# A gather ring of six slots instead of eight, and a half-chunk of query weights kept on chip between token blocks, in a two-layer decoder trunk

## The chip, the cores and the metric

The kernel runs on one core of a Trainium2 chip. The metric is the device time in microseconds (us) of one execution, all inputs in HBM, weights included. The kernel before took 1610.29 us in the median of three runs (1610.21, 1610.29 and 1612.72).

## The reference

A trunk of two layers runs over 256 tokens of width 1024, all in float32. Layer 0 mixes tokens with eight stick-breaking heads and four gated-linear-attention heads; layer 1 mixes them with a chunked gMLP gate (`c_w_in`, 1024 x 4096; a causal 128 x 128 matrix per group; `c_w_out`, 2048 x 1024). After each mixer comes a PEER block, and this is most of the work:

```
q = (h @ w_q)                                   # 1024 x 2048, 8 heads x 2 halves x 128
scores = einsum('thpd,hpnd->thpn', q, subkeys)  # 128 keys per half
top_s, top_i = top_k(scores, 16)                # per half, then the best 16 of the 16 x 16 sums
...
u_sel = u_tab[ii]                               # 128 experts per token, rows of 1024 floats
act = gelu(einsum('td,tkd->tk', xi, u_sel))
w = gi * act
out = einsum('tk,tkd->td', w, v_tab[ii])
```

Each token picks 128 of 16384 experts; of each it needs a row of `u` and a row of `v`, 8 KB together. Two layers and 256 tokens make 65536 such row pairs, 537 MB, gathered from HBM.

## The kernel before, in words

The 256 tokens are two blocks of 128, one token per partition. A *step* is one expert for each of a block's 128 tokens: 128 steps per block and layer, 512 in all, numbered 0 to 511 here over the four pairs (layer, block) = (0,0), (0,1), (1,0), (1,1). What a step does, engine by engine:

- POOL (L686) issues one indirect DMA that fetches 128 row pairs, 1 MB, into slot `t % SLOTS` of `ring` (8 slots of 8 KB per partition). Before it, POOL waits until step `t - SLOTS` has been used (`rows_used`), and in steps 2, 4, 6 and 7 of the whole kernel also for the end of what the prologue of layer 0 keeps in slots 4 to 7.
- DVE (L1229) multiplies the `u` half with the token's `h` and sums it to `dots`. It waits for all 16 parts of the DMA (`row_in`).
- ACT (L875, L876, L878) takes the gelu, multiplies by the gate and makes a diagonal 128 x 128 matrix of it.
- PE (L1580) multiplies that matrix with the `v` half into two PSUM banks, four matmul instructions, and counts `rows_used` up.

Everything else is placed between the steps by a list written out by hand, `PLAN`, which all five engines walk in the same order. `gather_with` puts stages behind given steps: the ranking of the next experts (`TOPK`, DVE), the query projection (`QPROD` and `QMORE`, PE) with its keys (`QDOT`), and layer 1's mixer (`ZPROJ`, `MIXG`, `MIXT`, `MIXO`), of which block 0 is computed behind the steps of (0,1) and block 1 behind those of (1,0). An engine never passes what stands ahead of it in this list.

Weights are streamed. A chunk is 1024 x 512 (2 MB), loaded by SP in two halves of 1 MB (`load_chunk`, L561). Each half goes to a *room* of 8 KB per partition: rooms 0 to 3 in `weights`, 4 in `scores1`, 5 and 6 in `z`, 7 and 8 in `more`. Rooms 4 to 8 are free only in parts of the plan (`spans`). `weight_rooms` walks the plan before the program is built and gives each half the room that has been free longest; SP then waits, in the order of the plan, until the last use of that room is over, and issues the load. A half listed in `kept` and `kept_halves` stays in its room (it is *pinned*) from block 0's use until block 1's, and block 1 then loads nothing. Kept so far are `ZPROJ` 2 and 3 and layer 1's query parts 2 and 3; layer 1's query parts 0 and 1 are loaded for each block anew. Layer 0's query parts serve both blocks from one load.

SP also loads the keys of layer 1 (`QKEYS`), after the last key product of layer 0, and nothing behind them in its order can be issued before.

Gathers (POOL's queue) and weight loads (SP's queue) are served by the same 16 DMA engines.

Of the kernel before, what the change touches and what calls it, by code (L numbers as in the profile page):

```python
# [5 lines left out]
P = 128  # L6
NBLK = 2
T = P * NBLK
D = 1024
KT = D // P  # L10
CH = 512
# [8 lines left out]
NEG = -1.0e30  # L20
LOWEST = -3.0e38

SLOTS = 8
STEPS = NE
PARTS = 4
PHEADS = PH // PARTS
# [1 line left out]
WB = 4  # L28
# [4 lines left out]
BATCHES = 6  # L33
# [54 lines left out]
ALL = tuple(range(PHEADS))  # L88
# [4 lines left out]
LOW_ROOMS = ((0, 1), (2, 3))  # L93
SCORES_ROOM, Z_HIGH_ROOM, Z_LOW_ROOM = 4, 5, 6
MORE_ROOMS = (7, 8)
N_ROOMS = 9
TK_PARTS = 6


# [186 lines left out]
def weight_rooms():  # L286

    places = {stage: at for at, stage in enumerate(PLAN)}
    last_mix = [max(places["MIXT", b, k] for k in range(4)) for b in range(NBLK)]
    spans = {SCORES_ROOM: [(places["TOPK", 0, 1, PH - 1, TK_PARTS - 1], places["VEC", "final", 0])]}  # L290
    for room in MORE_ROOMS:
        spans[room] = [(places["GLAREAD", 1], len(PLAN))]
    for room in (Z_HIGH_ROOM, Z_LOW_ROOM):
        spans[room] = [(last_mix[0], places["ZTAKE", 1, Z_ORDER[1][0]]), (last_mix[1], len(PLAN))]
    kept = {("ZPROJ", 1, 3): ("ZPROJ", 0, 3), ("ZPROJ", 1, 2): ("ZPROJ", 0, 2),
            ("QPROD", 1, 1, 2, ALL): ("QPROD", 1, 0, 2, ALL), ("QPROD", 1, 1, 3, ALL): ("QPROD", 1, 0, 3, ALL)}
    kept_halves = {("ZPROJ", 0, 3): (0, 1), ("ZPROJ", 0, 2): (0, 1), ("QPROD", 1, 0, 2, ALL): (0, 1), ("QPROD", 1, 0, 3, ALL): (0, 1)}
    again = {first: (later[0], later[1:]) for later, first in kept.items()}
    used_until, fills, pinned, homes = [-1] * N_ROOMS, [0] * N_ROOMS, set(), {}
    rooms, numbers, fresh = [], [], []  # L300
    for kind, args, at in walk():
        for i in range(chunks_of(kind, args)):
            name, n = (kind, *args), len(rooms)
            uses = half_uses(kind, args, places)
            place, number, new = [], [], []
            for half in range(2):
                if uses is None:
                    room, wait = 2 * (n % 2) + half, "used"
                    used_until[room] = places["OUT", 1, i, 3] if kind == "WOUT" else places[name]
                elif name in kept and half in kept_halves[kept[name]]:  # L310
                    room, wait = homes[kept[name]][half], None
                    pinned.discard(room)
                    used_until[room] = uses[half]
                else:
                    begin, end = places[name], uses[2 * i + half]
                    until = half_uses(*again[name], places)[half] if half in kept_halves.get(name, ()) else end
                    if kind == "MIXO" and i:
                        begin = places["OMORE", *args, 4]
                    choice = []
                    for r in range(N_ROOMS):  # L320
                        free_from, ok = used_until[r], r < SCORES_ROOM
                        for a, z in spans.get(r, ()):
                            if a < begin and until < z:
                                free_from, ok = max(free_from, a), True
                        if ok and free_from < begin and r not in pinned:
                            choice.append((free_from, r))
                    forced = name == ("ZPROJ", 0, 2) and half == 0
                    free_from, room = max(choice, key=lambda c: c[1]) if forced else min(choice)
                    wait = "used" if used_until[room] == free_from else "span"
                    used_until[room] = end  # L330
                if wait:
                    fills[room] += 1
                place.append(room)
                number.append(fills[room])
                new.append(wait)
                if half in kept_halves.get(name, ()):
                    pinned.add(room)
            rooms.append(place)
            numbers.append(number)
            fresh.append(new)  # L340
            homes[name] = place
    return rooms, numbers, fresh


ROOMS, FILLS, LOADS = weight_rooms()
# [6 lines left out]
BANKS = {}  # L352
# [7 lines left out]
def trunk(nc, x_in, cols, ab_w_in, ab_w_rank, ab_w_alpha2, ab_w_out, c_w_in, c_spatial, c_w_out,  # L360
# [6 lines left out]
    with ctx:  # L367
        def sb(name, shape, dt=f32):
            return ctx.enter_context(nc.sbuf_tensor(name, shape, dt))
# [8 lines left out]
        mixT = sb("mixT", [P, KT, T])  # L378
        weights = sb("weights", [P, 2, KT, CH])
        more = sb("more", [P, 2, KT // 2, CH])  # L380
        ring = sb("ring", [P, SLOTS, 2 * D])
        z = sb("z", [P, 2 * SGW])
        scores = sb("scores", [P, 2 * PH * NK])
        scores1 = sb("scores1", [P, 2 * PH * NK])
# [36 lines left out]
        def slots(k, n=1):  # L421
# [1 line left out]

        wide_rooms = [weights[:, i // 2, i % 2 * 4:i % 2 * 4 + 4, :] for i in range(4)] + [
            tile.rearrange("p (k n) -> p k n", n=CH) for tile in (scores1[:, :], z[:, SGW:2 * SGW], z[:, 0:SGW])] + [
            more[:, i] for i in range(2)]
        more_rows = more[:, :, :, :].rearrange("p a k n -> p (a k n)")
        first_chunk = z[:, :].rearrange("p (k n) -> p k n", n=CH)

# [30 lines left out]
        full = [sem(f"bank_full{k}") for k in range(WB)]  # L460
# [29 lines left out]
        sums_full = sem("sums_full")  # L490
# [50 lines left out]
        def _(sp):  # L541
# [6 lines left out]
            def load_chunk(n, src, used, block=0):  # L548

                for half in range(2):  # L550
                    room = ROOMS[n][half]
                    if LOADS[n][half] == "span" and room == SCORES_ROOM:
                        sp.wait_ge(experts_ready, 1 + IDS_ORDER[0, 1, PH - 1])
                    elif LOADS[n][half] == "span" and room in MORE_ROOMS:
                        sp.wait_ge(*filled(BANKS["GLAREAD", 1]))
                    elif LOADS[n][half] == "span":
                        sp.wait_ge(*filled(max(BANKS["MIXT", block, k] for k in range(4))))
                    elif LOADS[n][half] and room in room_used:
                        sp.wait_ge(*room_used[room])
                    if LOADS[n][half]:  # L560
                        sp.dma_start(wide_rooms[room], src[:, 4 * half:4 * half + 4, :]).then_inc(chunk_in[room], 16)  # L561
                    room_used[room] = used[half]

            for kind, args, at in walk():
# [43 lines left out]
                elif kind == "MIXO":  # L608
                    b, n = args
# [12 lines left out]
        def _(pool):  # L622
# [31 lines left out]
            for kind, args, at in walk():  # L654
                bank, chunk = at.bank, at.chunk
                if kind == "CAUSAL":
                    pool.wait_ge(spatial_in, 16)
                    pool.affine_select(out=spatialT[:, :, :], in_=spatialT[:, :, :], compare_op=ALU.is_ge, fill=0.0, base=0,
                                       pattern=[[0, SGG], [1, P]], channel_multiplier=-1).then_inc(spatial_masked, 1)
                elif kind == "GS":  # L660
                    for b in range(NBLK):
                        n = bank + b
                        pool.wait_ge(free[n % WB], n // WB + 1)

                        pool.affine_select(out=scT[:, b], in_=scT[:, b], compare_op=ALU.is_ge, fill=0.0, base=0,  # L665
                                           pattern=[[0, GH], [1, P]], channel_multiplier=-1).then_inc(scores_masked, 1)
                        pool.wait_ge(scores_masked, 2 * b + 1)
                        pool.memset(scT[0:GC, b, :, GC:P], 0.0).then_inc(scores_masked, 1)
                elif kind == "GATHER":
                    layer, b, i0, i1 = args  # L670
                    for step in range(i0, i1):
                        t = first_step(layer, b) + step
                        pool.wait_ge(experts_ready, 1 + IDS_ORDER[layer, b, step // TOPK])
                        if t == 2:
                            n = BANKS["GV", 1]
                            pool.wait_ge(full[n % WB], n // WB + 1)
                        elif t == 4:
                            pool.wait_ge(scores_full, BATCHES)
                        elif t == 6:
                            pool.wait_ge(sums_full, BATCHES)  # L680
                        elif t == 7:
                            n = BANKS["GLAREAD", 1]
                            pool.wait_ge(full[n % WB], n // WB + 1)
                        if t >= SLOTS:
                            pool.wait_ge(rows_used, t - SLOTS + 1)
                        pool.indirect_dma_start(  # L686
                            ring[:, t % SLOTS, :], None, uv_rows,
                            bass.IndirectOffsetOnAxis(ap=experts[:, b, step:step + 1], axis=0))\
                            .then_inc(row_in[t % SLOTS], 16)
# [964 lines left out]
```

## Time and profile before

| quantity | before |
|---|---|
| median of three runs | 1610.29 us |
| span of the profiled execution | 1611.4 us |
| PE, DVE, ACT, POOL busy | 89%, 61%, 41%, 41% |
| moved by DMA | 626.57 MB, mean 389 GB/s |
| gathers | 512 issues, 536.90 MB |
| loads and stores of the other queues | 89.6 MB |

The profiled execution's own time is given as its span, from its first instruction to the end of its last: 1611.4 us, inside the range of the three runs and 1.1 us over their median. The profile cuts the span into 40 slices of 40.3 us; in most of them from the fifth on DMA moves 421 or 422 GB/s.

### The profile page before, as it was taken

The numbers are of one execution on the slowest core, as the hardware profiler recorded it, in microseconds if no ns is written. First come the engines' busy times: TensorE is split into PE (matmuls) and PEld (weight loads), VectorE is DVE, ScalarE is ACT, GpSimd is POOL, SyncE is SP. The second block draws the span as 40 slices with busy tenths as digits, with TensorE's granted clock in tenths as the row PEclk, the third lists the DMA queues.
The fourth block names the chain that finished last, engine by engine and source line by source line (L and its number), as shares of the span: only waits on it lengthen the run. The fifth ranks groups of instructions, "written<-read, shape, count | busy, mean of one in ns | idle before, by whom it ended". The sixth has DMA issues, their size and how long they took to land.

```text
span 1611.4 us, 14849 instructions
## 1 busy us (share of the span) xinstructions
PE 1434.2 (89%) x4450; PEld 706.0 (44%) x4450; DVE 980.2 (61%) x2487; ACT 668.2 (41%) x1841; POOL 654.7 (41%) x535
## 2 busy tenths in 40 slices
PE   7999989999957998998988999999899889797776
PEld 6546455465412433443343545445335345342222
DVE  1226578758748756753347756566556778777744
ACT  1514544534525334442244534343334454444433
POOL 1001344444434333353345333333344544556673
PEclk9999999999989999999999999999999999999999
DMA  5443999999999999999999999999999999999996
GB/s 212 158 155 129 422 421 422 421 421 421 421 422 421 393 423 421 421 422 421 422 419 407 422 421 421 421 422 373 423 421 409 422 420 401 421 421 421 421 421 280
DMA packets 86656, 626.57 MB, mean 389 GB/s; under 512 B 9760, under 2 KB 9904, under 8 KB 10672
## 3 DMA queue, kind: packets, MB, share of 16 engines
q0 software_dynamic: 73728, 536.90, 80.6%
q1 hardware_dynamic: 12672, 88.45, 13.5%
q8 instruction: 35, 0.57, 0.1%
q14 instruction: 45, 0.37, 0.1%
q10 hardware_dynamic: 176, 0.28, 0.1%
HBM read 624.54 MB, written 1.05 MB: 388 GB/s over the span
## 4 chain that ended last, share of the span: by engine, by line
PE 42%; DMA 33%; DVE 10%; ACT 6%; issue 4%; POOL 3%; SPq 0%; POOLq 0%; DVEq 0%; ACTq 0%
DMA ring<-in_peer_uv,experts 33%; PE acc L1580 22%; DVE ring L1229 6%; PE work L1367 5%; PE work L1350 5%; POOL ring L686 3%; PE work L1339 3%; PE work L1382 2%; PE acc L1543 1%; ACT diag L878 1%; ACT gelus L876 1%; ACT L875 1%; PE work L1434 1%; ACT gelus L875 1%; ACT L869 1%
## 5 line engine op out<-in xcount | busy, mean ns | idle before, releaser
L1580 PE MATMUL acc<-ring,diag 128*128 128x512 f32 x2048 | 979.0, 612 | 158.7 <-ACT diag L878 156.6
L686 POOL DMA_INDIRECT ring<-in_peer_uv,experts x512 | 645.3, 1260 | 845.1 <-PE acc L1580 700.3
L1229 DVE CUSTOM_DVE_ANT_0 ring<-ring,h 128x1024 f32<-128x1024 f32 x512 | 624.9, 1226 | 440.4 <-DMA ring<-in_peer_uv,experts 427.8
L1580 PEld LDWEIGHTS acc<-ring,diag 128*128 128x128 f32 x2048 | 367.7, 191 | 687.5 <-ACT diag L878 349.5
L875 ACT ACTIVATE gelus<-dots 128x1 f32<-128x1 f32 x512 | 103.2, 201 | 694.5 <-DVE dots L1229 693.9
L878 ACT ACTIVATE diag<-ident,gelus 128x128 f32<-128x128 f32 x512 | 205.5, 401 | 16.7
L876 ACT ACTIVATE gelus<-gelus,gates 128x1 f32<-128x1 f32 x512 | 150.8, 295 | 16.6
L1350 PE MATMUL work<-weights,hT 128*128 128x512 f32 x192 | 88.1, 592 | 0.0
L1367 PEld LDWEIGHTS work<-hT,weights 128*128 128x128 f32 x576 | 69.8, 192 | 16.3 <-issue 16.3
L1367 PE MATMUL work<-hT,weights 128*128 128x128 f32 x576 | 70.1, 275 | 0.0
L1350 PEld LDWEIGHTS work<-weights,hT 128*128 128x128 f32 x192 | 36.2, 191 | 43.1 <-issue 43.0
L875 ACT ACT_TABLE_LOAD x41 | 52.6, 1283 | 0.7
L1350 PE MATMUL work<-more,hT 128*128 128x512 f32 x104 | 49.1, 594 | 0.0
L1339 PE MATMUL work<-hT,weights 128*128 128x256 f32 x192 | 43.5, 389 | 1.1 <-DMA weights<-in_ab_w_in 1.1
L1229 DVE DVE_READ_ACCUMULATOR2_ANT dots<- 128x1 f32 x512 | 42.2, 82 | 0.0
L1339 PEld LDWEIGHTS work<-hT,weights 128*128 128x128 f32 x192 | 37.6, 196 | 7.2 <-issue 1.9
L869 ACT ACT_TABLE_LOAD x31 | 39.8, 1283 | 0.5
L665 POOL TENSOR_SCALAR_AFFINE_SELECT more<-more 128x512 f32<-128x512 f32 x2 | 1.3, 630 | 88.1 <-ACT more L825 88.1
L1367 PEld LDWEIGHTS work<-hT,z 128*128 128x128 f32 x256 | 31.0, 192 | 7.2 <-issue 6.2
L1367 PE MATMUL work<-hT,z 128*128 128x128 f32 x256 | 31.6, 275 | 0.8 <-ACT hT L728 0.8
L1350 PEld LDWEIGHTS work<-more,hT 128*128 128x128 f32 x104 | 19.9, 193 | 24.5 <-issue 24.5
L1543 PE MATMUL acc<-weights,mixT 128*128 128x512 f32 x64 | 29.5, 595 | 0.8 <-DVE mixT L1181 0.8
(211 smaller groups left out, 898.3 us busy)
## 6 DMA issues: line engine op xcount, KB each, us to landing
weights<-in_c_w_in SPq DMA_DIRECT2D x14, 1024.0 KB, 9.1
more<-in_c_w_in SPq DMA_DIRECT2D x11, 1024.0 KB
weights<-in_ab_w_in SPq DMA_DIRECT2D x10, 1024.0 KB, 5.2
weights<-in_peer_w_q SPq DMA_DIRECT2D x10, 1024.0 KB, 9.2
ring<-in_peer_uv,experts POOLq DMA_INDIRECT x512
weights<-in_ab_w_out SPq DMA_DIRECT2D x4, 1024.0 KB, 5.2
weights<-in_c_w_out SPq DMA_DIRECT2D x4, 1024.0 KB, 12.2
scores<-in_c_w_out SPq DMA_DIRECT2D x4, 1024.0 KB
```

Of the source, the lines that this page charges most:

```text
L686: pool.indirect_dma_start(ring[:, t % SLOTS, :], None, uv_rows, bass.IndirectOffsetOnAxis(ap=experts[:, b, step:step + 1], axis=0))\
L869: nc.scalar.activation(g, g, ACT.Exp).then_inc(gate_exp, 1)
L875: link(nc.scalar.activation(gelus[:, k:k + 1], dots[:, k:k + 1], ACT.Gelu))
L876: link(nc.scalar.activation(gelus[:, k:k + 1], gelus[:, k:k + 1], ACT.Copy, scale=gates[:, b, step:step + 1]))
L878: nc.scalar.activation(diag[:, k, :], ident[:, :], ACT.Copy, scale=gelus[:, k:k + 1])\
L1229: nc.vector.tensor_tensor_reduce(out=ring[:, k, 0:D], in0=ring[:, k, 0:D], in1=h[:, b, :], scale=1.0, scalar=0.0, op0=ALU.mult, op1=ALU.ad ...
L1339: last = nc.tensor.matmul(dst, wt[k][:, t * P:(t + 1) * P], hT[:, k, cols], start=(k == 0), stop=(k == KT - 1))
L1350: last = nc.tensor.matmul(w[:, :], src[:, k, b * P:(b + 1) * P], wt[k], start=(k == 0), stop=(k == KT - 1))
L1367: last = nc.tensor.matmul(w[:, i * P:(i + 1) * P], wt[k][:, t * P:(t + 1) * P], hT[:, k, b * P:(b + 1) * P], start=(k == 0), stop=(k == KT ...
L1382: last = nc.tensor.matmul(w[:, :], mixT1[:, kh * KT + k % KT, :], wt[k % KT], start=(k == 0), stop=(k == 2 * KT - 1))
L1543: last = nc.tensor.matmul(acc[2 * b + n][:, :], mixT[:, k, b * P:(b + 1) * P], wt[k], start=(k == 0), stop=(k == KT - 1))
L1580: last = nc.tensor.matmul(acc[2 * b + n][:, :], diag[:, k, :], ring[:, k, D + n * CH:D + (n + 1) * CH], start=False, stop=True, skip_group ...
```

## The change

The ring has six slots. The two slots taken from it become rooms 9 and 10 for half-chunks of weights, free from stage `GLAREAD` 1 on (until then the prologue uses that memory, as before). The two halves of layer 1's query part 1 are kept from block 0 to block 1. The two waits of POOL that protected the old slots 6 and 7 go, and SP waits for `GLAREAD` 1 before the first fill of rooms 9 and 10. `dots`, `gelus`, `diag` and the semaphores `row_in` shrink to six with `SLOTS`.

```diff
-SLOTS = 8
+SLOTS = 6
+RING_ROOMS = 2
...
-N_ROOMS = 9
+SLOT_ROOMS = (9, 10)
+N_ROOMS = 11
...
-    for room in MORE_ROOMS:
+    for room in MORE_ROOMS + SLOT_ROOMS:
         spans[room] = [(places["GLAREAD", 1], len(PLAN))]
...
-    kept = {("ZPROJ", 1, 3): ("ZPROJ", 0, 3), ("ZPROJ", 1, 2): ("ZPROJ", 0, 2),
+    kept = {("QPROD", 1, 1, 1, ALL): ("QPROD", 1, 0, 1, ALL), ("ZPROJ", 1, 3): ("ZPROJ", 0, 3), ("ZPROJ", 1, 2): ("ZPROJ", 0, 2),
             ("QPROD", 1, 1, 2, ALL): ("QPROD", 1, 0, 2, ALL), ("QPROD", 1, 1, 3, ALL): ("QPROD", 1, 0, 3, ALL)}
-    kept_halves = {("ZPROJ", 0, 3): (0, 1), ...
+    kept_halves = {("QPROD", 1, 0, 1, ALL): (0, 1), ("ZPROJ", 0, 3): (0, 1), ...
...
-        ring = sb("ring", [P, SLOTS, 2 * D])
+        ring = sb("ring", [P, SLOTS + RING_ROOMS, 2 * D])
...
-            more[:, i] for i in range(2)]
+            more[:, i] for i in range(2)] + [
+            ring[:, SLOTS + i, :].rearrange("p (k n) -> p k n", n=CH) for i in range(RING_ROOMS)]
...
-                    elif LOADS[n][half] == "span" and room in MORE_ROOMS:
+                    elif LOADS[n][half] == "span" and room in MORE_ROOMS + SLOT_ROOMS:
                         sp.wait_ge(*filled(BANKS["GLAREAD", 1]))
...
                         elif t == 4:
                             pool.wait_ge(scores_full, BATCHES)
-                        elif t == 6:
-                            pool.wait_ge(sums_full, BATCHES)
-                        elif t == 7:
-                            n = BANKS["GLAREAD", 1]
-                            pool.wait_ge(full[n % WB], n // WB + 1)
                         if t >= SLOTS:
                             pool.wait_ge(rows_used, t - SLOTS + 1)
```

## Rows read from the trace of the kernel before

**Rows 1.** The page, parts 1 and 2: busy time; GB/s in 40 slices.
```profile
PE 1434.2 (89%) x4450; PEld 706.0 (44%) x4450; DVE 980.2 (61%) x2487; ACT 668.2 (41%) x1841; POOL 654.7 (41%) x535
...
GB/s 212 158 155 129 422 421 422 421 421 421 421 422 421 393 423 421 421 422 421 422 419 407 422 421 421 421 422 373 423 421 409 422 420 401 421 421 421 421 421 280
```
**Rows 2.** The page, part 3: DMA queues, packets, MB, share of 16 engines.
```profile
q0 software_dynamic: 73728, 536.90, 80.6%
q1 hardware_dynamic: 12672, 88.45, 13.5%
```
**Rows 3.** The page, part 4: the chain that ended last, by engine.
```profile
PE 42%; DMA 33%; DVE 10%; ACT 6%; issue 4%; POOL 3%; SPq 0%; POOLq 0%; DVEq 0%; ACTq 0%
```
**Rows 4.** Timeline of DVE in the last stretch: start, us, form [idle before, releaser].
```profile
1549.60 1.22 DVE L1229 CUSTOM_DVE_ANT_0 ring<-ring,h 128x1024 f32<-128x1024 f32 x1 [1.26 <-DMA ring<-in_peer_uv,experts]
...
1552.08 1.22 DVE L1229 CUSTOM_DVE_ANT_0 ring<-ring,h 128x1024 f32<-128x1024 f32 x1 [1.25 <-DMA ring<-in_peer_uv,experts]
```
**Rows 5.** Timeline of POOL in the same stretch.
```profile
1554.64 1.97 POOL L686 DMA_INDIRECT ring<-in_peer_uv,experts  x1 [0.52 <-issue]
```
**Rows 6.** Timeline of SP around 1180 us.
```profile
1171.29 8.91 SPq L561 DMA_DIRECT2D z<-in_peer_w_q  x2
1188.46 0.33 SPq L561 DMA_DIRECT2D scores<-in_peer_w_q  x1
```
**Rows 7.** The page, part 6: KB each, median us from issue to landing.
```profile
weights<-in_ab_w_out SPq DMA_DIRECT2D x4, 1024.0 KB, 5.2
```
**Rows 8.** Windows around 540 us: length, busy of PE, PEld, DVE, ACT, POOL, PEclk, DMA, GB/s.
```profile
538.50:539.50 1.00, 1.00 (x4) 0.51 (x3) 0.93 (x2) 0.98 (x2) 0.42 (x1) 1.00 0.45 188
539.50:542.40 2.90, 2.90 (x9) 1.23 (x8) 2.83 (x7) 2.79 (x6) 0.80 (x1) 1.00 0.99 364
542.40:543.40 1.00, 1.00 (x4) 0.52 (x3) 0.86 (x6) 0.89 (x4) 0.14 (x1) 1.00 0.52 164
```
**Rows 9.** Timeline of POOL in five stretches: the late issues.
```profile
260.39 1.65 POOL L686 DMA_INDIRECT ring<-in_peer_uv,experts  x1 [2.05 <-PE acc L1580]
...
537.98 0.94 POOL L686 DMA_INDIRECT ring<-in_peer_uv,experts  x1 [4.58 <-PE acc L1580]
541.60 0.94 POOL L686 DMA_INDIRECT ring<-in_peer_uv,experts  x1 [2.68 <-PE acc L1580]
...
1107.30 1.89 POOL L686 DMA_INDIRECT ring<-in_peer_uv,experts  x1 [2.11 <-PE acc L1580]
...
1238.16 1.49 POOL L686 DMA_INDIRECT ring<-in_peer_uv,experts  x1 [2.57 <-PE acc L1580]
...
1333.41 1.96 POOL L686 DMA_INDIRECT ring<-in_peer_uv,experts  x1 [9.04 <-PE acc L1580]
```
**Rows 10.** Timeline of DVE in the same stretches: starts that a landing released.
```profile
264.98 1.23 DVE L1229 CUSTOM_DVE_ANT_0 ring<-ring,h 128x1024 f32<-128x1024 f32 x1 [1.25 <-DMA ring<-in_peer_uv,experts]
...
519.84 1.23 DVE L1229 CUSTOM_DVE_ANT_0 ring<-ring,h 128x1024 f32<-128x1024 f32 x1 [0.84 <-DMA ring<-in_peer_uv,experts]
...
1095.82 1.23 DVE L1229 CUSTOM_DVE_ANT_0 ring<-ring,h 128x1024 f32<-128x1024 f32 x1 [0.18 <-DMA ring<-in_peer_uv,experts]
...
1112.23 1.22 DVE L1229 CUSTOM_DVE_ANT_0 ring<-ring,h 128x1024 f32<-128x1024 f32 x1
...
1237.61 1.22 DVE L1229 CUSTOM_DVE_ANT_0 ring<-ring,h 128x1024 f32<-128x1024 f32 x1 [1.25 <-DMA ring<-in_peer_uv,experts]
...
1337.63 1.23 DVE L1229 CUSTOM_DVE_ANT_0 ring<-ring,h 128x1024 f32<-128x1024 f32 x1 [0.54 <-DMA ring<-in_peer_uv,experts]
```
**Rows 11.** Windows of the trunk stages, the same columns.
```profile
550.00:721.00 171.00, 162.17 (x407) 72.77 (x406) 107.99 (x280) 71.98 (x199) 68.49 (x57) 0.99 1.01 421
721.00:824.00 103.00, 88.72 (x210) 37.21 (x207) 40.40 (x68) 32.47 (x100) 39.59 (x33) 0.98 1.01 421
...
1190.00:1226.00 36.00, 31.05 (x103) 15.72 (x103) 21.03 (x40) 16.47 (x46) 15.23 (x12) 0.95 1.01 421
```
**Rows 12.** Waits of PE between 565 and 1250 us, longest first.
```profile
PE acc L1580 <- ACT diag L878: 52.5, 53, 3.0
```

More of the change, by code:

```diff
@@ L294, in weight_rooms @@
         spans[room] = [(last_mix[0], places["ZTAKE", 1, Z_ORDER[1][0]]), (last_mix[1], len(PLAN))]
-    kept = {("ZPROJ", 1, 3): ("ZPROJ", 0, 3), ("ZPROJ", 1, 2): ("ZPROJ", 0, 2),
+    kept = {("QPROD", 1, 1, 1, ALL): ("QPROD", 1, 0, 1, ALL), ("ZPROJ", 1, 3): ("ZPROJ", 0, 3), ("ZPROJ", 1, 2): ("ZPROJ", 0, 2),
             ("QPROD", 1, 1, 2, ALL): ("QPROD", 1, 0, 2, ALL), ("QPROD", 1, 1, 3, ALL): ("QPROD", 1, 0, 3, ALL)}
-    kept_halves = {("ZPROJ", 0, 3): (0, 1), ("ZPROJ", 0, 2): (0, 1), ("QPROD", 1, 0, 2, ALL): (0, 1), ("QPROD", 1, 0, 3, ALL): (0, 1)}
+    kept_halves = {("QPROD", 1, 0, 1, ALL): (0, 1), ("ZPROJ", 0, 3): (0, 1), ("ZPROJ", 0, 2): (0, 1), ("QPROD", 1, 0, 2, ALL): (0, 1), ("QPROD", 1, 0, 3, ALL): (0, 1)}
     again = {first: (later[0], later[1:]) for later, first in kept.items()}
```

## The prediction

> **What bounds the kernel now.** I read the page's parts 1 and 2 first. PE is busy 89% of the span, which looks like the bound, but the line of GB/s says otherwise: from the fifth slice of 40.3 us to the last but one it stands at 421 or 422, whatever stage the plan is in, with dips in a few slices only [rows 1]. Nothing computes at so even a rate; this is the rate at which DMA can go here, and 1 MB (1.0486 million bytes) takes 1.0486 / 0.421 = 2.49 us. The gathers are 536.9 of the 625.4 MB of the two big queues, the weights most of the rest [rows 2]. The chain of waits gives PE 42% and DMA 33% [rows 3]; it hops between the two because each gather waits for a matmul to free its slot and each matmul for a gather. So I looked at one turn of this loop in the last stretch, where little else runs. DVE starts 2.49 us apart, each time released by a landing [rows 4]. Step 491 lands at 1549.60 and POOL issues the gather that reuses its slot at 1554.64: 5.04 us for dot product, diagonal matrix, matmuls and release. The issue itself stands there 1.97 us [rows 5]. A turn of eight slots is 8 x 2.49 = 19.9 us, so 19.9 - 5.04 - 1.97 = 12.9 us lie between the end of an issue and its landing, five transfers' time. The queue is deep, and DMA alone sets the end. Every byte less is time less, as long as DMA never waits for an issue.
>
> **The change, part by part.**
>
> *Two loads less.* Layer 1's query part 1 is no longer loaded for block 1. Its halves are the second of the two loads issued from 1171.29 us on and the one at 1188.46 [rows 6] (the first of the pair still belongs to part 0). They lie in the saturated stretch: 2 x 2.49 = 5.0 us gained.
>
> *Two more rooms.* In layer 0 the weights can come two halves earlier, in layer 1 the two new rooms are outweighed by the two pinned halves. The same bytes go through the same engines, only earlier; I cost it at nothing, and what it costs if PE minds is a rival below. SP's order is unchanged, and behind the key load of layer 1 nothing can be issued early anyway. POOL loses two waits near step 6. There gather 6 will wait for step 0 instead, some 6 us later than before; the two halves that now come with the first loads after the prologue keep DMA busy meanwhile, and PE is behind there, not DMA. Nothing.
>
> *The shorter ring.* A turn is now 6 x 2.49 = 14.9 us. In the last stretch 14.9 - 5.04 - 1.97 = 7.9 us are left from issue to landing. What is the least that does? A transfer of 1 MB to idle DMA engines lands 5.2 us after its issue starts [rows 7], of which the issue takes 0.3: 4.9 us is one end. The other comes from 540 us, where before already most DMA engines had run dry: POOL's issue ends at 538.92 (the row of 537.98 in [rows 9]), DMA is at half rate until about 539.5, busy for 2.9 us, and falls to half again at 542.4 [rows 8]. The gather's data were through 3.5 us after the end of the issue, and the signal comes after that. I take 4.2, the middle. So in the last stretch nothing is lost (4.2 against 7.9), and DMA runs dry only where PE frees a slot late.
>
> Where is that? The dips of [rows 1] mark four places (the slices from 524, 1088, 1209 and 1329 us), and I went through POOL's issues for more. In the shorter ring the slot freed at a given moment takes the gather two numbers lower, so an issue of before, with its time, now carries the gather two before it. It is late if the end of the issue + 4.2 lies after the time at which that lower gather landed before. POOL's rows are [rows 9], landings [rows 10], counted on by 2.49 us a step where DVE was late and does not show them:
> - Step 40 issued 260.39 + 1.65 + 4.2 = 266.2; step 38 landed at 264.98: 1.3 us late.
> - Step 144: 541.60 + 0.94 + 4.2 = 546.7; step 142, ten after the landing at 519.84, at 544.7: 2.0. The next issues are late by no more, since SP issues a weight half in this place, and its transfer fills the hole.
> - Step 330: 1107.30 + 1.89 + 4.2 = 1113.4; step 328, by pace 1110.8, at the latest when DVE took it, 1112.2: 1.2 to 2.6. The slice holds the deepest dip, so landings were behind the pace: 1.2.
> - Step 371: 1238.16 + 1.49 + 4.2 = 1243.9; step 369 at 1237.61 + 5.0 = 1242.6: 1.3.
> - Step 408: 1333.41 + 1.96 + 4.2 = 1339.6; step 406 at 1337.63: 1.9.
>
> Each hole shifts all later landings, which gives the engines behind a rest but is never won back; between the places PE catches up, so the next starts from zero and the five add: 7.7 us. With 3.5 us in place of 4.2 it would be 4.2 us; with 4.9, and 2.6 at step 330, it would be 12.6 plus some 1.5 for four or five issues that stand just short of late: 14.1.
>
> **Sum.** -5.0 + 7.7 = +2.7 us, between -0.8 and +9.1. The profiled execution's span, 1611.4, lies 1.1 over the median of the runs; the sum is a difference, small against both, so I put it on the median: 1610.3 + 2.7 = **1613.0 us**.
>
> **The rivals.**
>
> *The idle engine is served sooner, and most of the saving stays.* POOL's rows are 0.94 us long in some places and up to 1.96 in others [rows 9]. If the long ones only report the work late, a gather lands 0.94 + 3.5 = 4.4 us after its start, however long the row. Then the five places give 0, 1.3, 0, 0 and 0.2: 1.5 us lost, -5.0 + 1.5 = -3.5, **1606.8 us**. For it: the dip at 540 is served fast. Against it: the landing signal must come after the last byte, and 5.2 for the loads is longer. The Trainium skill, page "DMA: Bandwidth & Descriptors", section "Anatomy of one DMA — SWDGE (gpsimd) path", speaks for this side: about 2.0 us fixed plus bytes / 436 GB/s, 4.4 us for 1 MB, mostly the receipt of the last write. The 5.2 us of rows 7 are 0.8 longer than that rule gives.
>
> *The ring is too shallow in more places.* Places near the limit decide: the time from landing to reissue may be at most 14.9 - 4.2 less the issue's 0.9 to 2. If a restart takes 4.9 us or more, or if the pauses make PE fall to the half clock, the near places open too: +9 and more, **1619.4 us**. For it: DMA already thins out in five slices with eight slots. Against it: a thin slice is made of engines ahead of the others, and landings kept their pace.
>
> *The trunk is PE's.* From 550 to 721 us PE is busy 162.2 of 171.0, from 721 to 824 88.7 of 103.0, and 31.1 of 36.0 just after the loads that go [rows 11]. Weights that come earlier leave a stretch of bare gathers at 2.49 us a step later, where PE has less time for its projections; and the pinned halves may make a later half wait. PE waits today in these stages for nothing but the diagonal matrices [rows 12], so it has no stall of this kind that could shrink. If the 5 us taken from around 1180 are not all slack of PE's, up to those 5 us come back on top: -5.0 + 7.7 + 5.0, **1618 us**.
>
> **How the numbers follow.** 0.2% (3.2 us) is what a measurement of this kernel can tell from no change. Forecast 0.52, own range 1609.5 to 1617; first rival 0.25; second 0.15; third 0.08. Faster by over 3.2 us: nearly all of the first rival and a sliver of the forecast, 0.24. Within 3.2: two thirds of the forecast and the rest of the first rival, 0.36. Slower by over 3.2: the rest, 0.40. The range from 1606 to 1620 takes in the first rival's time and the upper bound.
>
> **What would show it.** In the last stretch issue to landing should be near 7.9 us and landings 2.49 apart. DMA bytes fall by 2.1 MB to 624.5. GB/s falls at the same five places, more than before, and DVE starts behind landings there instead of behind its own work. I am wrong if the last stretch itself goes slower than 2.49 us a step (the least from issue to landing is then over 7.9), if dips appear in slices that had none, or if PE shows waits for weights.

## The result, and the profile after

The changed kernel takes 1630.76 us (median of four runs, 1630.07 to 1633.46) against 1611.51 for the kernel before in the same comparison. The ratio is 1.0123, 95% interval 1.0111 to 1.0135: 19.2 us slower. The forecast was 1613.0 us, with a range to 1620. The direction was given the largest chance, the size was wrong by a factor of seven. Two of the eleven executions of `keep_one` below (1678.90 and 2536.88 us) were slow ones at a lower granted clock; they are left out of its time and ratio.

The page of the changed kernel, the lines that answer to [rows 1 to 3]:

```profile
PE 1442.2 (89%) x4450; PEld 707.1 (43%) x4450; DVE 981.9 (60%) x2487; ACT 669.1 (41%) x1841; POOL 660.5 (41%) x535
...
GB/s 209 170 141 158 420 392 394 422 413 409 421 422 404 390 422 421 421 406 420 422 420 422 363 423 417 422 421 373 422 415 382 419 392 364 422 412 416 421 421 313
...
q1 hardware_dynamic: 12384, 86.35, 13.1%
...
PE 45%; DMA 28%; DVE 12%; ACT 5%; issue 5%; POOL 5%; SPq 0%; POOLq 0%; DVEq 0%; ACTq 0%
```

The engines' work is the same. The two loads are gone: 2.1 MB less on the second queue. But the even row of 421 GB/s has more holes: from the fifth slice to the last but one, seventeen lie under 420 GB/s where there were six, and the chain goes less through DMA and more through engines. Dips in slices that had none (392 and 394 in the sixth and seventh from the start) were one of the forecast's signs of being wrong. The loads of layer 1's query weights near 1180 us, against [rows 6] (timeline of SP):

```profile
1170.97 0.33 SPq L564 DMA_DIRECT2D ring<-in_peer_w_q  x1
1181.24 0.33 SPq L564 DMA_DIRECT2D z<-in_peer_w_q  x1
```

Two half-chunks where there were four in this part of the plan; those of part 1 are no longer there.

The last stretch is as forecast. DVE starts 2.49 us apart on landings, and 5.04 us after the first of these POOL reuses its slot (timelines of DVE and of POOL; [rows 4, 5] before):

```profile
1564.91 1.23 DVE L1227 CUSTOM_DVE_ANT_0 ring<-ring,h 128x1024 f32<-128x1024 f32 x1 [1.24 <-DMA ring<-in_peer_uv,experts]
1567.40 1.23 DVE L1227 CUSTOM_DVE_ANT_0 ring<-ring,h 128x1024 f32<-128x1024 f32 x1 [1.25 <-DMA ring<-in_peer_uv,experts]
```

```profile
1569.95 1.97 POOL L684 DMA_INDIRECT ring<-in_peer_uv,experts  x1 [0.52 <-issue]
```

The issue ends at 1571.92, its gather lands six steps after 1564.91, at 1579.8: 7.9 us, the number of the forecast, at full pace. So the time went elsewhere. I compared the moment at which DVE starts the same step in the profiled executions (differences to before, us; from step 120 on the change also carries its loads at another time):

| step (before, us) | six slots alone | the change | my sum's holes up to here |
|---|---|---|---|
| 0 (155.1) | 0.6 | -1.4 | 0 |
| 50 (294.8) | 5.1 | 4.0 | 1.3 |
| 120 (489.0) | 4.7 | 9.7 | 1.3 |
| 150 (572.9) | 7.7 | 12.0 | 3.3 |
| 230 (824.8) | 7.0 | 5.6 | 3.3 |
| 250 (874.2) | 9.1 | 10.8 | 3.3 |
| 320 (1091.3) | 8.5 | 10.0 | 3.3 |
| 340 (1159.9) | 11.5 | 12.6 | 4.5 |
| 360 (1220.2) | 10.7 | 7.0 | 4.5 |
| 380 (1270.9) | 12.8 | 11.2 | 5.8 |
| 391 (1300.1) | 12.9 | 11.3 | 5.8 |
| 420 (1373.8) | 19.9 | 18.2 | 7.7 |
| 511 (1601.7) | 18.7 | 17.8 | 7.7 |

The losses are stairs, and they stand where my five places stand: near the start, at the first and the third change of block (steps 128 and 384), and around steps 328 and 371. With six slots alone each stair is 1.5 to 4 times as high as I had it. One more, from step 230 to 250, stands at none of them. The difference of the last row is 17.8 us with the change, like that of the spans (1629.2 - 1611.4). It is less than the medians' 19.2, mostly because the profiled execution of the kernel before, timed at 1612.72 us, was 1.2 us over its median. A lag counted in steps also moves when weight loads come earlier or later, so it does not only show lost time: the change's lag falls from 12.0 to 5.6 us between steps 150 and 230.

The last big stair, at step 406, in the timelines of POOL and DVE of the changed kernel ([rows 9, 10] before):

```profile
1348.40 1.75 POOL L684 DMA_INDIRECT ring<-in_peer_uv,experts  x1 [9.27 <-PE acc L1578]
```

```profile
1335.34 1.23 DVE L1227 CUSTOM_DVE_ANT_0 ring<-ring,h 128x1024 f32<-128x1024 f32 x1 [0.89 <-DMA ring<-in_peer_uv,experts]
...
1354.81 1.22 DVE L1227 CUSTOM_DVE_ANT_0 ring<-ring,h 128x1024 f32<-128x1024 f32 x1 [2.95 <-DMA ring<-in_peer_uv,experts]
```

Step 400 lands at 1335.3, its slot is reused 13.1 us later (POOL sat idle for 9.27 us, waiting for PE), the issue ends at 1350.15, and step 406 lands at 1354.8. From the end of the issue that is 4.66 us, 0.46 more than my 4.2, on engines that had nothing else to do. From step 400 to 406 it took 19.5 us, where six transfers are 14.9.

The same place in the run `ring6_less` (below) has a shorter row of POOL:

```profile
1346.66 1.00 POOL L684 DMA_INDIRECT ring<-in_peer_uv,experts  x1 [8.87 <-PE acc L1578]
```

```profile
1352.31 1.22 DVE L1227 CUSTOM_DVE_ANT_0 ring<-ring,h 128x1024 f32<-128x1024 f32 x1 [1.79 <-DMA ring<-in_peer_uv,experts]
```

Here the row is 1.00 us long and step 406 lands 4.65 us after its end. With rows of 1.75 and of 1.00 us the time from the end of the issue is the same, that from its start is not (6.41 and 5.65 us).

### The profile page after: what moved, and what is told of

Read it like the earlier page. It is cut to its first block, busy times and chain, and to the rows that moved or that the text cites. A ratio compares the mean times of both kernels' runs of the same rounds, so it can differ in the third digit from the quotient of the medians.

```text
span 1629.2 us, 14847 instructions
## 1 busy us (share of the span) xinstructions
PE 1442.2 (89%) x4450; PEld 707.1 (43%) x4450; DVE 981.9 (60%) x2487; ACT 669.1 (41%) x1841; POOL 660.5 (41%) x535
## 3 DMA queue, kind: packets, MB, share of 16 engines
q1 hardware_dynamic: 12384, 86.35, 13.1%
## 4 chain that ended last, share of the span: by engine, by line
PE 45%; DMA 28%; DVE 12%; ACT 5%; issue 5%; POOL 5%; SPq 0%; POOLq 0%; DVEq 0%; ACTq 0%
DMA ring<-in_peer_uv,experts 27%; PE acc L1578 24%; DVE ring L1227 6%; PE work L1348 6%; PE work L1365 5%; POOL ring L684 5%; PE work L1337 3%; PE work L1380 2%; ACT diag L876 1%; ACT gelus L874 1%; PE work L1432 1%; PE acc L1541 1%; PE work L1319 1%; ACT L873 1%; ACT gelus L873 1%
## 5 line engine op out<-in xcount | busy, mean ns | idle before, releaser
L1348 PE MATMUL work<-weights,hT 128*128 128x512 f32 x200 | 92.8, 597 | 0.0
L1365 PEld LDWEIGHTS work<-hT,weights 128*128 128x128 f32 x352 | 43.4, 194 | 8.6 <-issue 8.6
L1365 PE MATMUL work<-hT,weights 128*128 128x128 f32 x352 | 44.2, 276 | 0.0
L1365 PEld LDWEIGHTS work<-hT,more 128*128 128x128 f32 x288 | 37.0, 196 | 10.9 <-issue 10.9
L1348 PE MATMUL work<-ring,hT 128*128 128x512 f32 x88 | 41.4, 592 | 0.0
L1337 PEld LDWEIGHTS work<-hT,weights 128*128 128x128 f32 x192 | 36.4, 190 | 6.6 <-issue 1.8
L1365 PE MATMUL work<-hT,more 128*128 128x128 f32 x288 | 37.5, 279 | 0.0
L1113 DVE TENSOR_TENSOR scores<-scores,topf 128x256 f32<-128x256 f32 x64 | 27.2, 426 | 2.2
```

What stands on the lines that cost most here:

```text
L1337: last = nc.tensor.matmul(dst, wt[k][:, t * P:(t + 1) * P], hT[:, k, cols], start=(k == 0), stop=(k == KT - 1))
L1348: last = nc.tensor.matmul(w[:, :], src[:, k, b * P:(b + 1) * P], wt[k], start=(k == 0), stop=(k == KT - 1))
L1365: last = nc.tensor.matmul(w[:, i * P:(i + 1) * P], wt[k][:, t * P:(t + 1) * P], hT[:, k, b * P:(b + 1) * P], start=(k == 0), stop=(k == KT ...
```

## Experiments

**Taking the change apart.** Four kernels. Six slots alone, as an edit of the change (the memory of the other two slots is left unused after the prologue):

```diff
-N_ROOMS = 11
+N_ROOMS = 9
...
-    for room in MORE_ROOMS + SLOT_ROOMS:
+    for room in MORE_ROOMS:
...
-    kept = {("QPROD", 1, 1, 1, ALL): ("QPROD", 1, 0, 1, ALL), ("ZPROJ", 1, 3): ...
+    kept = {("ZPROJ", 1, 3): ...
```

> Six gather slots and nothing else: the memory of the two slots stays unused after the prologue, and layer 1's query part 1 is loaded for both blocks. Theory A (depth: a gather needs about 7.5 us from the end of its issue to its landing, not 4.2, or DMA loses time): the ring alone costs what the change lost plus the 5.0 us of the loads, 19 + 5 = 24, so 1635 us. Theory B (rooms: the earlier loads and the pinned halves cost the surplus over my sum, the ring alone only its 7.7 us): 1619 us.

Measured: 1631.11 us against 1611.50, ratio 1.0123 (1.0107 to 1.0138). The ring alone costs 19.6 us. That is not the 24 of theory A and not the 7.7 of theory B: by the medians the ring alone is as slow as the change, and nothing is seen of the saved loads. (`dots`, `gelus` and `diag` have six places as well, but they can't hold a step up: gather `t` is issued only after PE has used step `t - 6`, and with it its places in all three.)

Two loads less on eight slots. Here and in `ring6_less` a part of the scores comes from other weights, so other experts are fetched, but as many bytes of them. The edit of the kernel before:

```diff
-    kept = {("ZPROJ", 1, 3): ...
+    kept = {("QPROD", 1, 1, 1, ALL): ("QPROD", 1, 1, 0, ALL), ("ZPROJ", 1, 3): ...
-    kept_halves = {("ZPROJ", 0, 3): (0, 1), ...
+    kept_halves = {("QPROD", 1, 1, 0, ALL): (0, 1), ("ZPROJ", 0, 3): (0, 1), ...
```

> Eight slots as before, but layer 1's query part 1 of block 1 uses the weights of part 0 that are still on chip, so its two half-chunk loads are left out and that part of the scores is computed from other weights. Both theories: two transfers of 2.49 us less, 1606.5 us. If it is 1610 or more, the loads were hidden or PE took their time back near 1190 us.

Measured: 1606.60 against 1611.50, ratio 0.9970 (0.9959 to 0.9982): -4.9 us. The first term of my sum holds to a tenth, where the ring is deep. The same edit on six slots:

> Six slots, the room plan of before, and the two half-chunk loads of layer 1's query part 1 for block 1 left out (it uses part 0's weights, still on chip, so part of the scores is computed from other weights). Six slots alone took 1631.1 and the change 1630.8, so the 5.0 us of the loads have gone. If the rooms and pins took them (theory B), this run keeps them: 1626 us. If the shorter ring gives them back wherever gathers come faster after the missing loads (theory C: with six slots PE's lateness sets the pace behind 1190 us, not bytes), it stays near 1630 us.

Measured: 1629.31 us against 1611.39, ratio 1.0119 (1.0103 to 1.0134). By the medians that is 1.8 us under six slots alone, not 4.9, with the room plan of before in both, which is theory C's side. But the executions of each kernel lie 3.7 or 3.8 us apart and the two intervals overlap, and the traces speak against it. SP's loads are the same in both up to the missing ones. The profiled execution of `ring6_less` starts step 340 2.1 us after that of six slots alone, step 360 2.5 us before it, and step 511 3.9 us before it. So 4.6 us are gained where the loads are missing, as on eight slots (5.1 in the same 20 steps), and none of it is lost behind. Whether six slots pass the gain on is open; a loss of it is not shown.

Six slots with the two new rooms, but everything loaded twice (the change without its new entries in `kept` and `kept_halves`):

> Six slots, the two new rooms in use, query part 1 loaded for both blocks. Theory B: the rooms' earlier loads cost about 5 us, 1636 us. Theory C: the rooms cost nothing, 1631 us.

Measured: 1634.56 us (1631.37 to 1637.11), ratio 1.0143 (1.0128 to 1.0159). So the rooms cost about 3.4 us and keeping part 1 gives 3.8 back. The runs of one such kernel lie up to 6 us apart and the interval overlaps that of six slots alone, so neither number is clear of the noise. Together: 19.6 + 3.4 - 3.8 = 19.2, as it must be, since all are differences of the same medians.

One thing that the rooms do can be read. Eight half-chunks of layer 1 follow the key load at once, where the kernel before issues six (timeline of SP, changed kernel):

```profile
444.58 0.33 SPq L602 DMA_DIRECT2D keysT<-in_peer_keys  x1
444.95 0.91 SPq L564 DMA_DIRECT2D weights<-in_c_w_in  x2
445.90 0.91 SPq L564 DMA_DIRECT2D more<-in_c_w_in  x2
446.85 0.90 SPq L564 DMA_DIRECT2D ring<-in_c_w_in  x2
447.80 0.90 SPq L564 DMA_DIRECT2D weights<-in_c_w_in  x2
```

The gathers are held up two transfers, 5 us, longer. The table shows it in the column of the change, from 4.0 at step 50 to 9.7 at step 120, and by step 230 it is made up for.

**How much depth costs what.** Seven slots and five slots, with nothing else changed (from the change; rooms and `kept` as in six slots alone):

```diff
-SLOTS = 6
-RING_ROOMS = 2
+SLOTS = 7
+RING_ROOMS = 1
```

> Seven slots and nothing else. A turn is 17.4 us. By my sum (4.2 us from issue to landing is enough) no issue would be late any more, 1611 to 1612 us. Theory A: with 7.5 us needed, a slot may be released 9 us after its landing at most; the same places as in the change show, each about 2.5 us milder: 1618 us (1615 to 1622).

Measured: 1613.12 us against 1611.50, ratio 1.0009 (1.0000 to 1.0018): 1.6 us, near nothing, under theory A's 1615 to 1622 and just over my sum's 1612. (POOL keeps the wait in step 6 there, for the prologue's data in the seventh slot.)

> Five slots and nothing else. A turn is 12.4 us, and in the last stretch 12.4 - 5.0 - 2.0 = 5.4 us are left from issue to landing. By my sum's 4.2 us the last stretch keeps its 2.49 us a step and only the late places grow, by 2.5 us each and some more places, about 1645 us. Theory A (7.5 us needed): landings in the last stretch are more than 2.49 us apart, at 7.5 us as a hard limit (5.0 + 2.0 + 7.5) / 5 = 2.9 us, and the kernel takes 1690 us or more.

Measured: 1725.62 us, ratio 1.0696 (1.0676 to 1.0715). The series for 8, 7, 6 and 5 slots is 0, +1.6, +19.6 and +114 us. My 1645 for a least time of 4.2 us is refuted by this run already: its last 100 steps take 23 us longer than with eight, where by 4.2 us they would have lost nothing.

**Where it costs.** Eight slots in memory, but POOL waits longer before it issues in chosen steps, so that the queue is six (or five) deep there only, with no other change:

```diff
+SHALLOW = ((16, 50), (128, 152), (256, 280), (384, 412))
...
-                            pool.wait_ge(rows_used, t - SLOTS + 1)
+                            shallow = any(a <= t < z for a, z in SHALLOW)
+                            pool.wait_ge(rows_used, t - SLOTS + 1 + 2 * shallow)
```

> Eight slots, but POOL waits two steps longer before it issues the gathers of steps 16 to 49, 128 to 151, 256 to 279 and 384 to 411 (that is, six deep there alone: the start and the three changes of block). Theory A: the loss of six slots sits where the plan crowds the steps, and these four stretches hold about two thirds of it, +12 us, 1623 us (1619 to 1627). If the loss were a general slowing of a shallow queue, a fifth of the steps would bring a fifth of it, 1615 us.

Measured: 1621.02 us (1620.65 to 1621.73) against 1611.39, ratio 1.0064 (1.0050 to 1.0078): +9.6 us, half of the loss in a fifth of the steps. Counted as in the table, its lag is 5.8 us at step 50, rises by 1.5 from 140 to 150 and by 7.5 from 391 to 420; the change of block at step 256 cost it next to nothing. Between the stretches the lag falls, from 5.8 at step 50 to 2.1 at 391, and it ends at 7.6.

> Eight slots, six deep only from step 412 on, where hardly anything lies between the steps. Theory A: from issue to landing 7.9 us are left there, more than the gather needs, and nothing is lost: 1611 us (to 1613). A general slowing: again about a fifth of the loss, 1615 us.

Measured: 1611.51 us, ratio 1.0004 (0.9995 to 1.0013). Six deep costs nothing where the plan is empty. A general slowing of a short queue is out. In `depth6_edges` the longer wait alone, in the memory of before, brought half of the loss. No run waited six deep in all 512 steps, so it is likely but not shown that depth is the whole of the 19.6 us.

> Eight slots, six deep only for steps 384 to 411, the third change of block. My sum of before has one hole there, 1.9 us: 1613.3 us. The trace of six slots alone loses 6 us there: 1617.5 us.

Measured: 1617.63 us (1614.24 to 1619.33), ratio 1.0037 (1.0023 to 1.0051): +5.8 us for 28 steps, three times my 1.9. The trace is of its fastest execution, in which the lag grows by 4.2 us from step 391 to the end. It has two stairs of 2.4 us, at steps 393 and 406, and a smaller one near 416, most of which is made up for later. I had only the second. The first is instructive (timelines of POOL and DVE, then windows with the columns of [rows 8]):

```profile
1293.15 1.33 POOL L688 DMA_INDIRECT ring<-in_peer_uv,experts  x1 [2.57 <-PE acc L1582]
```

```profile
1298.21 1.22 DVE L1231 CUSTOM_DVE_ANT_0 ring<-ring,h 128x1024 f32<-128x1024 f32 x1
1302.60 1.23 DVE L1231 CUSTOM_DVE_ANT_0 ring<-ring,h 128x1024 f32<-128x1024 f32 x1 [3.16 <-DMA ring<-in_peer_uv,experts]
```

```profile
1286.00:1292.50 6.50, 6.29 (x32) 3.99 (x31) 6.19 (x21) 2.88 (x10) 1.57 (x2) 1.00 1.01 425
1297.00:1301.00 4.00, 4.00 (x23) 2.72 (x21) 2.43 (x6) 2.00 (x7) 1.45 (x1) 1.00 0.93 295
```

The issue of step 393 ended at 1294.48, while step 392 was still on its way; DVE took 392 at 1298.21. By my rule 393 should have landed 2.49 us after 392. It landed at 1302.6, 8.1 us after the end of its issue. In these 4 us the DMA engines are busy for 93% of the time, yet move 295 GB/s instead of 421 x 0.93 = 392: they are not idle, their packets take longer. In the trace single packets of 8 KB take up to 2.3 us there against 0.31 in the even stretches.

Five deep, only from step 412 on (`SHALLOW = ((412, 512), )` and `3 * shallow`):

> Eight slots, five deep only from step 412 on, in the stretch where six deep lost nothing. 5.4 us are left there from the end of an issue to its landing in the steady loop. If 4.2 us are enough, as my sum had it: 1612 us. If a gather needs 6.6 us, which is what the late ones took in the last stretch of five slots: a turn is 5.0 + 1.0 to 2.0 + 6.6 = 12.6 to 13.6 us against 12.4, 0.04 to 0.24 us a step over 100 steps, and more where something stands between the steps: 1611.5 + 4 to 24, I expect 1630 us.

Measured: 1638.17 us (1637.31 to 1639.93), ratio 1.0164 (1.0150 to 1.0178): +26.3 us, where 4.2 us as the least time gives nothing and 6.6 gave 4 to 24, of which I expected 19. The timelines of POOL and DVE show a gather in the steady loop:

```profile
1560.43 1.92 POOL L688 DMA_INDIRECT ring<-in_peer_uv,experts  x1 [0.53 <-issue]
```

```profile
1565.48 1.23 DVE L1231 CUSTOM_DVE_ANT_0 ring<-ring,h 128x1024 f32<-128x1024 f32 x1 [1.25 <-DMA ring<-in_peer_uv,experts]
1569.17 1.22 DVE L1231 CUSTOM_DVE_ANT_0 ring<-ring,h 128x1024 f32<-128x1024 f32 x1 [2.46 <-DMA ring<-in_peer_uv,experts]
```

Step 490 is issued until 1562.35, 3.1 us before 489 lands, and lands itself 3.7 us after that: 6.8 us from the end of its issue, and 1.2 us lost. The gathers before and behind it differ: 489 had only 5.6 us from the end of its issue to its landing, and landed at full pace. Over 85 us of this stretch (columns of [rows 8]):

```profile
1505.00:1590.00 85.00, 64.10 (x124) 22.21 (x124) 47.00 (x103) 30.84 (x97) 38.85 (x31) 0.96 0.98 381
```

The DMA engines are busy for 98% of the time and move 381 GB/s. With six deep (`depth6_bare`) the same 85 us show 422. So the slower packets of step 393 are no single event.

**Is it PE's lateness?** Six slots alone, PE's second product cut:

```diff
+                            cols = CH if n == 0 else 64
-                            last = nc.tensor.matmul(acc[2 * b + n][:, :], diag[:, k, :],
-                                                    ring[:, k, D + n * CH:D + (n + 1) * CH],
+                            last = nc.tensor.matmul(acc[2 * b + n][:, 0:cols], diag[:, k, :],
+                                                    ring[:, k, D + n * CH:D + n * CH + cols],
```

> Six slots alone, and in every step the second of PE's two products takes 64 columns instead of 512, so most of the second half of the PEER output is left out. PE's work of a step falls from about 2.4 to 1.4 us and it frees slots earlier, above all where it is behind; DMA moves the same bytes. Theory A: the loss of six slots needs PE to be late, so most of the 19.7 us goes, 1615 us (1612 to 1620). If a queue of six is slow by itself, 1630 us.

Measured: 1621.79 us (1619.47 to 1627.85), ratio 1.0068 (1.0052 to 1.0085): 10.5 us over the kernel before. A little under half of the 19.6 us went, less than expected. The run does not separate cleanly. PE's busy time fell from 1440 us with six slots alone to 1259, by 181 us and not by some 500 (1.0 us in each of 512 steps) as expected. It was granted half the clock for 402 us of the span, against 39 with six slots alone:

```profile
PE 1259.0 (78%) x4450; PEld 733.5 (45%) x4450; DVE 982.8 (61%) x2487; ACT 670.2 (41%) x1841; POOL 595.9 (37%) x535
```

And DVE's and ACT's crowded stages stay. PE's lateness carries a part; how much of the rest is DVE's and ACT's is open.

**Taking a crowd apart.** The changed kernel with the final norm of block 0 spread over the plan:

```diff
-normed(14, "final", 0) + [(16, ("STORE", 0))]
+[(14, ("NORM", "final", (0,))), (18, ("VEC", "final", 0)), (23, ("NMEAN", "final", 0)),
+ (28, ("NSCALE", "final", 0)), (28, ("STORE", 0))]
```

> The changed kernel with one edit of the plan: the four stages of block 0's final norm, which stand behind steps 14 to 16 of (1,1) (steps 398 to 400) and hold DVE while ACT and PE hand the values on, are spread to steps 14, 18, 23 and 28. Theory A (six slots lose where one engine's crowded stages delay the release): the hole near step 406 shrinks, 5 us less than the change, 1626 us. If the loss there comes from the ring in another way, the time stays at 1631.

Measured: 1632.46 us (1630.24 to 1636.91), ratio 1.0122 (1.0107 to 1.0138): no gain. In its trace steps 391 to 412 fall behind by 1.1 us where the change loses 6.5, but then 2.9 more are lost up to step 420, where the values are now handed on, and the profiled execution was 9 us behind the change's by step 376 (8 of them already at step 50), in a part of the plan that is the same in both. So kernels with six slots vary by several us from one execution to the next, and this run can't show 3 us. It is no proof for or against the remedy.

**Two attempts at a faster kernel.** Seven slots cost 1.6 us and free room for one half:

> Seven slots, the eighth as one more room, and one half of query part 1 kept. Seven slots alone cost 1.6 us; one transfer less gives 2.5. By these two 1610.5 us. As at six slots (rooms +3.4, two halves kept only -3.8 of 5.0) part of it is lost again: 1612 us.

Measured: 1617.65 us (1615.65 to 1620.66), ratio 1.0036 (1.0023 to 1.0049). Worse than seven slots alone by 4.5. The waits of PE show a likely cause, one wait for a half-chunk of `ZPROJ` weights in the new room; the kernel before had none for weights there [rows 12]:

```profile
PE work L1350 <- DMA ring<-in_c_w_in: 7.3, 1, 7.3
```

Another room and another pin change the whole rotation of rooms behind them, and one half came late.

One half kept on eight slots, in the nine rooms of before (`kept_halves` with `(0,)` for part 1; with both halves `weight_rooms` finds no room):

> Eight slots and the nine rooms of before; one half of layer 1's query part 1 is kept until block 1, pinned in the old rooms. One transfer less: 1609.0 us, if the two rooms that are then left for the stream of layer 1's weights suffice. If they don't, PE shows waits for weights and it is at 1611 us or over.

Measured: 1609.88 us against 1611.33, ratio 0.9988 (0.9978 to 0.9997): 1.4 us faster, where 2.3 were expected (1609.0). It is the one version with all its weights that beats both kernels, by little: the edit of `kept` without the shorter ring.

## Why the prediction was wrong

- **What bounds the kernel**: right. DMA sets the pace, PE's 89% is not the bound, and bytes taken away on a deep ring come off the time one for one (-4.9 for 5.0).
- **Two loads less**: the term of -5.0 was right on eight slots. On six the medians give -1.8 (`ring6_less`) and -3.8 (the change against `ring6_rooms`), neither clear of the noise, and the trace of `ring6_less` keeps the whole gain. Open.
- **More rooms cost nothing**: 3.4 us on six slots by two medians, within the spread of these kernels. Not settled.
- **The last stretch loses nothing**: right (7.9 us from issue to landing; `depth6_bare` 0). The step that lands at 1549.60 is 490, not 491; the slot of 490 is the one that the issue at 1554.64 reuses, so the 5.04 us stand.
- **The five late places**: this is the step that failed. I priced them at +7.7 us, and six slots alone cost 19.6. Of the 16.5 us between forecast and result 11.9 lie here, the rest is 3.4 for the rooms and 1.2 for the loads, both within the noise. The places were right: with the landings of the trace in place of my counted ones, my rule gives 1.3, 2.1, 1.3, 1.3 and 2.0. What failed is the rule itself, that a gather lands at full pace as long as 4.2 us are left from the end of its issue.
  - 4.2 was too low even for idle engines. I took the middle between 3.5 and 4.9. The 4.9 was a load of SP's queue. The 3.5 was read from the dip at 542.4; but of that gather, step 143, fifteen parts landed 3.9 to 5.0 us after the end of its issue and the last 10.2. Step 406 takes 4.66.
  - With a thin queue the time is not fixed. In the trace of six slots alone the shortest gathers at full pace take 4.6 to 4.8 us (steps 34, 81, 366, 407). Others come late after 6.8 us (step 490 of `depth5_bare`) and 8.1 (step 393 of `depth6_last`), while the rate is below 421 GB/s.
  - So more places count than five. I read four dips in [rows 1]; there is a fifth, 407 GB/s in the slice from 846 us on, and six slots alone lose 2.1 us from step 230 to 250, which is there. Step 393 is another (2.4 us in `depth6_last`).
  - With 6.6 instead of 4.2 the same five would give 7.7 + 5 x 2.4 = 19.7 us. That this is the measured 19.6 is luck: by the same rule three more places (the gathers of steps 81, 244 and 396) would open by 2.0 to 2.2 us each, some 26 us in all, and single gathers did land at full pace with less than 6.6.
- **"Never won back"** was said too strongly: in `depth6_edges` the lag of 5.8 us at step 50 was 2.1 at step 391.
- **Where the sum could have warned me**: after the start no gather in the trace before took less than 7.5 us from the end of its issue to its landing (step 408: 1335.38 to 1342.91). Everything below that was ground no row covered, and I bounded it by rows of another situation, nearly idle engines. The top of my range, +9.1, stood on the same footing and was too low.
- **The rivals**: the second one, "too shallow in more places", is what happened, at twice its price. Its half-clock branch is not the cause: six slots alone were granted 0.989 of the clock on average, as before (0.989). The first rival, served sooner, is refuted at step 406: 6.41 us from the start of the issue, not 4.4, and it is the end of POOL's row that counts (4.66 us behind a row of 1.75, 4.65 behind one of 1.00). The rule of the Trainium skill that stood beside it ("DMA: Bandwidth & Descriptors", section "Anatomy of one DMA — SWDGE (gpsimd) path", 2.0 us fixed plus the bytes, by which I had estimated 4.4 us) is 1.2 to 2 us short here for one gather to idle engines, and 4 to 5 us short for steps 490 and 393 in a thin queue. The third, PE in the trunk, is not shown: PE waits for no weights there in the change, and in `ring6_less` nothing came back behind the missing loads.

## What to carry to other kernels

A ring in front of a saturated DMA has a reserve that can be read from the trace: slots times transfer time, less the time from landing to reissue at its worst, less the issue. Compare it with the shortest issue-to-landing time at which the trace keeps full pace throughout (here 7.5 to 7.9 us), not with the latency of a transfer to idle engines: single gathers made it in 4.6 to 5.5, but the kernels in which many had less than 7.5 lost time. Expect a cliff rather than a slope (0, +1.6, +19.6, +114 us for 8, 7, 6 and 5 slots). To price a shorter buffer before building it, make the producer wait longer in chosen steps with the memory unchanged: that is one line, and it shows the place as well as the cost.

## What the runs showed of the hardware

- DMA engines with little in their queues move less even while they are busy. In `depth6_last`, busy 93% of 4 us, they moved 295 GB/s, with single 8 KB packets of up to 2.3 us instead of 0.31; in `depth5_bare`, busy 98% of 85 us, 381 GB/s where 422 is full pace, with packets of up to 1.9 us. What holds the packets up, no run here tells; it is open.
- The 16 parts of one gather don't land together. Of step 142 of the kernel before, 15 had landed between 537.8 and 541.4 us and the last at 544.7. In the even stretches the last part came 2 to 4 us after the fifteenth (median), and DVE waits for it. So DMA could stand at half rate from 542.4 us on [rows 8] while landings still kept their pace up to step 142: most engines were ahead, the last one was not. The Trainium skill ("DMA: Bandwidth & Descriptors", section "Latency and other measured facts") says that DMA engines 7 and 15 are usually slower; the trace agrees that the engines differ, but does not name the one that lags.
- Work cut from PE came back as a lower granted clock. In `ring6_narrow` PE was busy 78% of the span instead of 88%, and the granted clock was at the lower of its two levels for 402 us, a quarter of the span, instead of 39.
